# Attention loops of a two-block transformer kernel: the weight turns of a pair's two heads side by side, the filling matmuls of both gaps behind them

## The reference, cut to what matters

```python
def one_block(qblk):                                       # first block: 8 + 8 heads, no mask
    s = jnp.einsum("bqhgd,bkhd->bhgqk", qblk, k).astype(jnp.float32)
    pr = jax.nn.softmax(s, axis=-1).astype(v.dtype)
    return jnp.einsum("bhgqk,bkhd->bqhgd", pr, v)
...
def fox_attention(q, k, v, log_f):                         # second block, even layer: 8 heads, causal
    s = s + (Fb.transpose(0, 2, 1)[..., :, None] - F_keys[..., None, :])
    s = jnp.where(key_pos[None, :] <= q_pos[:, None], s, -jnp.inf)
    p = jax.nn.softmax(s, axis=-1)
    return jnp.einsum('bhqk,bkhd->bqhd', p.astype(v.dtype), v)
...
def dsa_attention(...):                                    # second block, odd layer: 16 heads, causal,
    s = s + bias.transpose(0, 1, 3, 2).astype(jnp.float32) # top-k of an index score, bias by distance
    p = jax.nn.softmax(s, axis=-1)
```

## Time and profile before

| | |
|---|---|
| median of 3 runs | 1352.04 us (1351.71 to 1353.36) |
| the profiled execution: its time | 1353.35 us |
| its span (first to last instruction) | 1351.4 us |
| granted TensorE clock, mean | 0.999 |
| PE busy | 1334.4 us, 99% of the span |
| DVE busy | 969.5 us, 72% |
| ACT busy | 678.4 us, 50% |
| loop "first" in the span | about 73 to 133 us |
| loop "fox" | about 618 to 657 us |
| loop "odd" | about 1099 to 1150 us |

### The profile page before, as it was taken

The page is one execution under the profiler, slowest core; times in us unless marked ns, Lnnn a source line. Parts: engine busy times, 40 slices in busy tenths (PEclk is TensorE's granted clock), DMA queues, the critical chain, the costliest instruction groups (busy, mean ns, idle before and its releaser), DMA issues.

```text
span 1351.4 us, 19410 instructions
## 1 busy us (share of the span) xinstructions
PE 1334.4 (99%) x7680; PEld 1145.0 (85%) x7680; DVE 969.5 (72%) x1324; ACT 678.4 (50%) x1057; POOL 71.4 (5%) x110
## 2 busy tenths in 40 slices
PE   8999999999999999999999999999999999999998
PEld 6988888888888888898888888888888887888886
DVE  5886777666687767657767766776676798676775
ACT  6586453444554444556644444544443667544442
POOL 0300010000000000004000000000000044000000
PEclk9999999999999999999999999999999999999999
DMA  8353556555546555464446555466554545565551
GB/s 315 133 170 112 187 167 230 195 188 188 187 126 218 200 193 194 150 203 125 136 158 210 194 192 195 164 200 197 194 188 165 185 136 147 176 209 196 187 187 47
DMA packets 67594, 241.31 MB, mean 179 GB/s; under 512 B 7999, under 2 KB 8392, under 8 KB 67504
## 3 DMA queue, kind: packets, MB, share of 16 engines
q1 hardware_dynamic: 65200, 234.19, 52.3%
q0 software_dynamic: 2016, 5.77, 1.7%
q10 hardware_dynamic: 288, 0.11, 0.0%
HBM read 238.88 MB, written 1.09 MB: 178 GB/s over the span
## 4 chain that ended last, share of the span: by engine, by line
PE 84%; DVE 10%; DMA 2%; ACT 2%; issue 2%; POOL 0%; DVEq 0%; POOLq 0%; SPq 0%; ACTq 0%
PE pp L466 82%; DVE wlo L1727 4%; PE pp L475 2%; DMA raw<-w_chunks 2%; DVE fa L1727 1%; DVE pbuf L1731 1%; ACT whi L1273 1%; DVE xn L1936 1%; DVE hx L1735 1%; DVE fa L1827 0%; DVE fa L1735 0%; DVE fa L2307 0%; DVE xn L1727 0%; ACT hx L1274 0%; DVE st L2303 0%
## 5 line engine op out<-in xcount | busy, mean ns | idle before, releaser
L1727 DVE TENSOR_TENSOR wlo<-raw,whi 128x1024 fp32r<-128x1024 f32 (+1 forms) x444 | 522.9, 1220 | 140.8 <-ACT whi L1273 140.6
L466 PE MATMUL pp<-hx,whi 128*128 128x512 f32 (+1 forms) x2400 | 541.2, 360 | 2.1 <-DVE fa L1827 1.1
L1273 ACT ACTIVATE whi<-raw 128x1024 fp32r<-128x1024 f32 (+1 forms) x444 | 441.9, 1043 | 83.4 <-PE pp L466 74.5
L466 PEld LDWEIGHTS pp<-hx,whi 128*128 128x128 f32 x2400 | 419.6, 188 | 73.8 <-issue 7.9
L466 PE MATMUL pp<-whi,ra 128*128 128x512 f32 x1144 | 366.2, 391 | 0.0
L466 PE MATMUL pp<-hx,wlo 128*128 128x256 f32 x2032 | 314.2, 278 | 0.0
L466 PEld LDWEIGHTS pp<-hx,wlo 128*128 128x128 f32 x2032 | 278.3, 188 | 10.0
L466 PEld LDWEIGHTS pp<-whi,ra 128*128 128x128 f32 x1144 | 214.6, 188 | 43.7 <-issue 0.9
L466 PE MATMUL pp<-wlo,ra 128*128 128x512 f32 x572 | 222.7, 389 | 0.0
L1827 DVE TENSOR_REDUCE fa<-pp 128x512 f32<-128x1024 f32 x104 | 127.0, 1221 | 73.3 <-PE pp L466 73.2
L1273 ACT ACTIVATE ra<-fa 128x512 fp32r<-128x512 f32 x63 | 39.8, 632 | 228.0 <-DVE fa L1735 228.0
(11 more groups left out here) (176 smaller groups left out, 768.7 us busy)
## 6 DMA issues: line engine op xcount, KB each, us to landing
raw<-w_chunks SPq DMA_DIRECT2D x438, 512.0 KB, 5.2
fa<-t_rows POOLq DMA_DIRECT2D x16, 128.0 KB, 3.4
fx<-x_t SPq DMA_DIRECT2D x2, 512.0 KB, 6.7
X<-x_in SPq DMA_DIRECT2D x2, 512.0 KB, 8.5
fa<-g_fin POOLq DMA_DIRECT2D x2, 512.0 KB, 4.3
fa<-f_rows POOLq DMA_DIRECT2D x8, 128.0 KB, 3.2
raw<-w_chunks SPq DMA_DIRECT2D x3, 256.0 KB, 6.2
cst<-consts POOLq DMA_DIRECT2D x1, 576.0 KB, 7.5
```

What stands on the lines that cost most here:

```text
L466: return pe.matmul(o, lhs, rhs, start=first, stop=last, skip_group_check=True)
L1273: return act.activation(o, i, ACT.Copy, scale=1.0)
L1727: return dve.tensor_tensor(o, a, b, op)
```

## The change

`fill` takes several places and does their steps one behind the other. In the turn of the loop, the transposes of head 2p-1 now follow those of head 2p-2 at once, and the steps of both gaps stand behind them. Nothing is added or removed, and the other engines' programs are the same row by row, waits included.

```diff
-                def fill(p, at):
-                    point[0] = (p, at)
-                    for _ in range(STEPS[name].get(p, USUAL[name])[at]):
-                        next(units, None)
+                def fill(p, *ats):
+                    point[0] = (p, ats[-1])
+                    for at in ats:
+                        for _ in range(STEPS[name].get(p, USUAL[name])[at]):
+                            next(units, None)
...
                     if 1 <= p <= pairs:
                         turn_weights(2 * p - 2)
-                        fill(p, 1)
                         turn_weights(2 * p - 1)
-                        fill(p, 2)
+                        fill(p, 1, 2)
                     ended[name, p, 1] = consumed[0]
```

## The result

The changed kernel takes 1355.72 us (median of 12 runs, 1355.15 to 1357.51); the kernel before, in 12 runs beside it and earlier, 1353.30 us (1351.71 to 1355.36). The ratio is 1.0020, with a 95% interval of 1.0012 to 1.0027: a small loss, clear of noise, 2.42 us between the medians. Forecast were +2.47 us, called "no change" because it lay inside 0.2%, and 1354.5 us, with a range of 1352.8 to 1356.0 that holds the measured time.

A forecast was written before the change was run, and what follows sets the result against it. TensorE, busy for 99% of the span, was taken to bound the kernel nearly everywhere. Terms 0 + 0 + 0.71 + 1.07 + 0.69 = +2.47 us on the median 1352.04 gave 1354.5 us, range 1352.8 to 1356.0.

The forecast's parts named there:

- The waits at the shared bank: Heads 4/5 and 6/7 of fox, 14/15 of odd: second head waits for ScalarE's copy; +0.71, +1.07, +0.69 us.
- The edges: Changes between transposes and filling matmuls on TensorE, in all loops: fewer of them gain nothing; 0 us, bounds 0 and -1.5.
- the first rival: Each change of kind costs 0.08 us, 16 are won (1.3 us), 0.8 us after absorption; 1353.7 us; chance 0.08.
- Head 3: Start of fox: late weights delay what follows by 0.35 us, which a later wait for ScalarE absorbs; 0 us.
- The later copy of head 6: Fox: ScalarE's copy before head 7 moves with the earlier 0.71 us and takes back none of it.
- The clock: Rival: at head 7, after 1.6 us of waiting, clock granted at half; +2.1 us, together +4.6, 1356.6; chance 0.05.
- The wait of 1.87 us in the prediction: TensorE's longest wait from 7 to 12 us of the span, where the granted clock is 1.00; cited against a clock fall.
- my own case: Whole kernel: sum of +2.47 us, chance 0.72, split 0.37 to same and 0.35 to slower.
- The level: Whole kernel: forecast time 1354.5 us, set against the runs' median of 1352.04 us; 0.18% more.

The follow-up runs named there:

- e2_only_shared: Kernel before, with turns put side by side only at the three pairs sharing one bank (fox turns 3 and 4, odd turn 8); ratio 1.0019 to before.
- e1_split_at_shared: Full change everywhere except at the three pairs sharing one bank, which keep their steps between the heads; ratio 0.9995 to the kernel before.
- e3_after_banks: Full change, with heads 5 and 15 turned into bank 4 and head 7 into bank 5; 1351.54 us, ratio 0.9988 to the kernel before.
- e8_all_between: Kernel before, but at the three shared-bank pairs all steps stand between the heads, none between second head and weigh; ratio 1.0009.

## Why the prediction was right in its sum and wrong in its call

- **The waits at the shared bank (three terms, +0.71, +1.07, +0.69).** Right: 0.70, 1.05, 0.69 in the trace of the changed kernel. e2_only_shared shows that these three places make the whole loss, e1_split_at_shared that nothing of it is left without them, e3_after_banks that it is the bank and no other reason to wait. The error of some 0.6 us that the prediction gave this sum was far too wide: it came out at 2.44. The waits before heads 5, 7 and 15 were forecast at 1.4, 1.6 and 0.8 us and are printed as 1.23, 1.47 and 0.67; the distances from start to start, less 0.33 for the transposes, are 1.39, 1.63 and 0.83, since the printed idle time begins at the modelled end of the last transpose.
- **The edges (0).** Right, against the 1.3 us of the first rival: 2.29 us before and after in turn 1 of "first". The loop as a whole is 0.16 us shorter, which I had not forecast. Some 0.05 of it is a wait of the weigh in each of the last two turns, whose copy now starts earlier; the rest is not traced to an instruction.
- **Head 3 (0).** Right in the term: what follows it comes late, and the next wait for ScalarE takes that up. From the transposes of head 2 to the scores behind the fill there are 635.06 - 632.21 = 2.85 us in place of 635.34 - 632.76 = 2.58, so 0.27 late where the prediction had 0.35. In the changed kernel the weigh of turn 3 starts at 636.01 without a wait, 5.08 us before head 4, and before the change at 636.61, also 5.08 before.
- **The later copy of head 6 moves along.** Right: 1.97 and 1.96 us between heads 6 and 7 in the two traces, though all before it had slipped by 0.70.
- **The clock.** It did not fall: the granted clock of the changed kernel is 0.999 over the span. From 649 to 655 us, which holds the wait of 1.47 us and the six steps behind it, it is 1.00, in the third value from the end here:

```profile
649.00:655.00 6.00, 4.53 (x40) 4.04 (x40) 5.89 (x8) 3.39 (x5) 0.00 (x0) 1.00 0.22 70
```

It is 1.00 over each of the three loops too. Nor does the clock explain the loss between the medians: over the 12 executions with the change its mean is 0.9977, over 78 executions of the kernel before, run beside the experiments, 0.9981. A line fitted to these 78 gives 0.7 us more for a clock lower by 0.001, so by this estimate the difference is worth some 0.3 of the 2.4 us. (The wait of 1.87 us in the prediction is the part that lies behind 7.00; TensorE's row at 8.87 prints the whole of it with 1.92.)

- **What failed** is the last step, the one from the sum to the call. "Within about 0.2% (2.7 us) a measurement of this kernel can hardly be told from no change, and the forecast lies just inside that": with 12 runs on each side the interval is 0.08% wide to either side, not 0.2%, and +2.47 us (0.18%) is a loss that it shows. No row stood behind the 0.2%: the one scatter on record was that of three runs, 1351.71 to 1353.36, which is 0.12% from the lowest to the highest. The sum had three losses, each on a row, and 0 for everything on the other side; from that "slower" follows, by little, and not "same". I gave "slower" 0.40 and "same" 0.57, and spread my own case over the bound as if its sign were open.
- The level, 1354.5 against 1355.72, is off by 1.2 us. It was built on 1352.04, the median of three runs; that of 12 runs is 1353.30, 1.26 higher. The difference was right to 0.05 us.

## What to carry to other kernels

When work that fills a gap is moved, ask of each gap what it covered: where two producers share a buffer, the distance between them is the way of the copy, as long as what stands between is shorter, and each filling step that leaves comes on top in full. Where they have a buffer each, the place of the fill was worth nothing here; so look for a free buffer first (here two score banks past their last use, -0.10% to -0.12%), then for the order. And if every term of a sum has the same sign and a row, forecast that sign even when the sum is small, and take the size that a measurement can show from the scatter of runs, not from a round number.

## What the runs showed of the hardware that I had not expected

Heads whose transposes stand in one block keep the pace of 0.11 us for a transpose of 128x128 in fp32, though the second head has two semaphore waits of its own: in turn 6 of "odd" of the changed kernel six in a row span 0.82 us, less 0.27 for the last one is 0.55 for five distances. From transposes to transposes through an idle ScalarE's copy of 128x384 there are 1.16 us, but from transposes to the weigh that reads the copy 1.07 (e8_all_between, three times): the way is not the same for each waiting instruction. The copy itself is printed with 0.49 us in both, and the difference lies behind its end. In "odd", turn 8, of the changed kernel the copy of head 14 ends at 1144.78 + 0.49 = 1145.27 and the transposes start at 1145.41, 0.14 later; in e8_all_between the copy of head 15 ends at 1146.49 + 0.49 = 1146.98 and the weigh starts at 1147.04, 0.06 later. What makes the 0.08 was not tried.
